# One softmax reciprocal per attention unit: from a power on GpSimd to a reciprocal on VectorE

## The chip, the core and the metric

The kernel runs on one core of a Trainium2 chip. The metric is the device time of one launch in microseconds. The profile names the engines PE (TensorE), DVE (VectorE), ACT (ScalarE), POOL (GpSimd) and SP (SyncE, which issues most transfers); PEld is PE's loading of weights.

## The reference

Two layers of a bidirectional encoder over 512 tokens of width 1024, in float32. Each layer has three token mixers side by side (A, B and C), an output projection, and an MLP. What matters here is the softmax of the mixers:

```python
def one_block(qblk):
    s = jnp.einsum('bhgqd,bhkd->bhgqk', qblk, k, preferred_element_type=jnp.float32) * scale
    p = jax.nn.softmax(s, axis=-1)
    return jnp.einsum('bhgqk,bhkd->bhgqd', p.astype(v.dtype), v)
```

C has 8 query heads (2 key heads), B has 4 heads, and A has 4 heads of dilated window attention with a bias; in the kernel A is a softmax over all 512 keys too, with the log of the count of windows that hold a key added to its bias. The output of the three goes through `w_o`, then a layer norm, then the MLP and a second layer norm.

## The kernel before, in words

The instruction streams of the engines are written out by hand and run in parallel; they meet at semaphores alone. A semaphore name such as `exped` counts up through the kernel, and a wait asks for a count. Each engine runs its stream in order: what stands behind a waiting instruction waits as well. An outer loop of two runs the layers.

Attention is a pipeline over 64 units a layer. A unit is one of 16 heads (C, then A, then B) with one of 4 tiles of 128 query rows. All matrices are split into a high and a low part, and products are summed from two or three passes. At step s of the pipeline:

- PE computes the scores of unit s into one of 3 banks (L1438, L1439, or L1284 to L1286 for B), transposes the probabilities of unit s-3 (L1451) once `normed` says that they are ready and once `pt_ready` of unit s-6 frees the bank, and does half of the product with the values for the two units s-6 and s-5 (L1284 to L1286, with the tiles pt_hi and pt_lo).
- DVE takes the negated row maximum of unit s from the bank (L1034); for A it adds the bias from the tile `band` and takes the maximum in one operation (L1027) and negates it (L1031). Then it makes pt_lo of unit s-4 from the transposed bank and pt_hi (L1041). Once in four steps each it also prepares the low part of the next head's q (L1012) and of k (L1005, where a new key head begins) and of v (L1057), and evacuates the head's output (L1049, "y part" below).
- ACT computes exp of unit s with the row sum as accumulator (L687, the sum in `smax[:, s % 4, 1:2]`), then pt_hi of unit s-3 (L695), and the high parts for q, k, v and the output.
- POOL waits for `exped`, raises the row sum to the power -1 (L450, against the constant tile `mone`), waits for its own result, multiplies the 128x512 tile of probabilities with it (L452) and signals `normed`.

`prob` and `smax` have 4 buffers each. The tile `band` has one, which SP loads for each of A's heads after the last maximum of the head before it. Around attention, PE works through weight slabs that ACT and DVE split into high and low parts.

Of the kernel before, what the change touches and what calls it, by code (L numbers as in the profile page):

```python
# [29 lines left out]
P = 128  # L30
KT = D // P
TT = S // P
# [44 lines left out]
UNITS = NH * TT  # L77
# [20 lines left out]
def trunk(nc, t_in, out, scratch):  # L98
# [3 lines left out]
    with ExitStack() as ctx:  # L102
# [37 lines left out]
        msq = keep("msq", [P, TT, 16])  # L140
        rms = keep("rms", [P, TT, 16])
        mhalf = keep("mhalf", [P, 16])
        mone = keep("mone", [P, 1])
        smax = keep("smax", [P, 4, 4])
        tmp = keep("tmp", [P, 2, S])
        u0 = cursor[0]
# [65 lines left out]
        def sem(name):  # L212
# [30 lines left out]

        k_hi_done, head_hi, head_ready, v_hi_done, v_ready = map(
            sem, ("k_hi_done", "head_hi", "head_ready", "v_hi_done", "v_ready"))
        scored, maxed, exped, normed, transposed, pt_hi_done, pt_ready, pv_done, y_hi_done, y_ready = map(
            sem, ("scored", "maxed", "exped", "normed", "transposed", "pt_hi_done", "pt_ready",
                  "pv_done", "y_hi_done", "y_ready"))
        h2_ready, acc_zero = sem("h2_ready"), sem("acc_zero")

# [145 lines left out]
        def _(pool):  # L396
            steps = [0]
# [8 lines left out]
            pool.memset(ones[:, :], 1.0).then_inc(setup_pool, 1)  # L406
            pool.memset(mhalf[:, :], -0.5).then_inc(setup_pool, 1)
            pool.wait_ge(setup_pool, 3)
            pool.memset(mone[:, :], -1.0).then_inc(setup_pool, 1)
            pool.affine_select(out=ident[:, :], in_=ones[:, :], compare_op=ALU.is_equal, fill=0.0, base=0,  # L410
                               pattern=[[-1, P]], channel_multiplier=1).then_inc(setup_pool, 1)
            pool.memset(lnrow[:, 0, :], 1.0).then_inc(setup_pool, 1)
            pool.memset(lnrow[:, 1, :], 0.0).then_inc(setup_pool, 1)
            pool.wait_ge(setup_pool, 7)
            PER = 2 * TT + TT + 2 * TT + UNITS + 2 * TT + 2 + 4
            with pool.Fori(0, DEPTH) as l:
                steps[0] = 0

# [26 lines left out]
                    j = 10 + n // TT  # L445
                    inv_sqrt(rms[:, n % TT, j:j + 1], msq[:, n % TT, j:j + 1], 1, brstd_done)
                for u in range(UNITS):
                    wait_apart(pool, exped, l * UNITS + u + 1)
                    p = prob[:, u % 4, :]
                    step(pool.tensor_tensor(smax[:, u % 4, 2:3], smax[:, u % 4, 1:2], mone[:, :], ALU.pow))  # L450
                    wait_apart(pool, pool_step, l * PER + steps[0])
                    pool.tensor_scalar(p, p, smax[:, u % 4, 2:3], 1.0, ALU.mult, ALU.mult).then_inc(normed, 1)  # L452
                for t in range(TT):
                    wait_apart(pool, var_ready, l * 8 + t + 1)
# [337 lines left out]
        def _(dve):  # L792
            steps = [0]
# [40 lines left out]
            with dve.Fori(0, DEPTH) as l:  # L834
# [181 lines left out]
                for s in range(ATT_STEPS):  # L1016
                    if s < UNITS:
                        m, h = HEADS[s // TT]
                        dve.wait_ge(scored, l * UNITS + s + 1)
                        if s >= 4:  # L1020
                            dve.wait_ge(exped, l * UNITS + s - 3)
                        if m == "A":
                            qt = s % TT
                            if qt == 0:
                                dve.wait_ge(band_in, (l * 4 + h + 1) * 16)
                            wait_apart(dve, transposed, l * UNITS + s - 3)
                            step(dve.tensor_tensor_reduce(prob[:, s % 4, :], bank[s % 3][:, :],  # L1027
                                                          band[:, 384 - P * qt:896 - P * qt], 1.0, -3.0e38,
                                                          ALU.add, ALU.max, smax[:, s % 4, 3:4]))
                            settle()  # L1030
                            dve.tensor_scalar(smax[:, s % 4, 0:1], smax[:, s % 4, 3:4], -1.0, None, ALU.mult  # L1031
                                              ).then_inc(maxed, 1)
                        else:
                            dve.tensor_reduce(smax[:, s % 4, 0:1], bank[s % 3][:, :], AX.X, ALU.max, negate=True  # L1034
                                              ).then_inc(maxed, 1)
                    u = s - LO_LAG
                    if 0 <= u < UNITS:
                        half = u // 2
# [209 lines left out]
        @block.tensor  # L1248
        def _(pe):
            pe.sem_inc(slab_free, RING)  # L1250
            pe.wait_ge(setup_pool, 5)

            def mod_cols(dst, src):

# [353 lines left out]
```

## Time and profile before

| | |
|---|---|
| median of 3 runs | 1533.49 us (1531.55 to 1535.78) |
| the profiled execution | 1535.78 us |
| its span in the profile | 1534.0 us |
| PE busy | 1347.1 us, 88% |
| DVE busy | 1080.8 us, 70% |
| ACT busy | 598.7 us, 39% |
| POOL busy | 360.4 us, 23% |

The span runs from the first to the last instruction that the profile shows. Busy shares are means over stages that have different limits, so the stretch in question has to be read by itself. In the chain of waits each piece is followed back from the last instruction to what released it; only work on that chain sets the end.

### The profile page before, as it was taken

How to read it: one execution, taken by the hardware profiler on the slowest of the kernel's cores; microseconds unless marked ns; L12 is line 12 of the kernel's file. 1: busy time of each engine (PE TensorE's matmuls, PEld its weight loads, DVE VectorE, ACT ScalarE, POOL GpSimd, SP SyncE). 2: the span in 40 equal slices, each digit the busy share in tenths (PEclk: the TensorE clock that was granted, in tenths of full speed). 3: DMA queues.
4: the chain of work that ended last, by engine and by line, in shares of the span. 5: the costliest groups of instructions: out<-in, count | busy, mean ns of one | idle time of the engine just before them, and what ended most of it. 6: DMA issues, size and time to landing. Idle time of an engine off the chain costs nothing.

```text
span 1534.0 us, 23304 instructions
## 1 busy us (share of the span) xinstructions
PE 1347.1 (88%) x6728; PEld 1133.7 (74%) x6728; DVE 1080.8 (70%) x1702; ACT 598.7 (39%) x1216; POOL 360.4 (23%) x411
## 2 busy tenths in 40 slices
PE   4598998899789999999929999979977999999992
PEld 2498777787668888887829977758766888888782
DVE  6957779877866555655777777988688655645668
ACT  0245478761422222221223647878132222222221
POOL 0504056540610000000361403756043000000024
PEclk9899989899889999999969999999998999999996
DMA  8654510104323332334325473010422333333431
GB/s 290 241 186 153 195 41 7 32 8 131 97 93 125 118 123 90 124 124 148 104 68 194 121 239 102 1 37 1 138 83 90 124 109 111 116 123 123 150 97 55
DMA packets 91844, 173.09 MB, mean 113 GB/s; under 512 B 8093, under 2 KB 18717, under 8 KB 91737
## 3 DMA queue, kind: packets, MB, share of 16 engines
q1 hardware_dynamic: 91208, 169.74, 34.2%
q10 hardware_dynamic: 528, 2.10, 0.4%
q8 instruction: 46, 0.75, 0.2%
q14 instruction: 62, 0.50, 0.1%
HBM read 167.61 MB, written 4.19 MB: 112 GB/s over the span
## 4 chain that ended last, share of the span: by engine, by line
PE 60%; DVE 18%; issue 10%; DMA 6%; ACT 3%; POOL 1%; DVEq 0%; SPq 0%; ACTq 0%; POOLq 0%
PE bank L1284 19%; PE bank L1285 19%; PE bank L1286 18%; DVE hT_hi L859 3%; DMA ada_w<-in_w_ada 2%; DVE ada_sum L807 1%; DVE slab_lo L851 1%; PE bank L1451 1%; DMA slab_raw<-in_w 1%; DVE smax L1034 1%; DVE pt_lo L1041 1%; DMA slab_raw<-in_w_in 1%; DVE X L1069 1%; DMA band<-bias_rows 1%; DVE tmp L1066 1%
## 5 line engine op out<-in xcount | busy, mean ns | idle before, releaser
L1284 PE MATMUL bank<-hT_hi,slab_hi 128*128 128x512 f32 x576 | 228.0, 396 | 22.9 <-DVE slab_lo L851 16.4
L1285 PE MATMUL bank<-hT_lo,slab_hi 128*128 128x512 f32 x576 | 226.5, 393 | 0.0
L1286 PE MATMUL bank<-hT_hi,slab_lo 128*128 128x512 f32 x576 | 226.3, 393 | 0.0
L1284 PE MATMUL bank<-slab_hi,h_hi 128*128 128x512 f32 x512 | 201.0, 393 | 6.3 <-ACT mod_a L778 6.3
L1286 PE MATMUL bank<-slab_hi,h_lo 128*128 128x512 f32 x512 | 199.4, 389 | 0.0
L1285 PE MATMUL bank<-slab_lo,h_hi 128*128 128x512 f32 x512 | 199.3, 389 | 0.0
L1284 PE MATMUL bank<-slab_hi,hT_hi 128*128 128x384 f32 (+3 forms) x448 | 155.8, 348 | 38.2 <-DVE slab_lo L851 20.2
L1121 DVE TENSOR_TENSOR slab_lo<-slab_raw,slab_hi 128x512 fp32r<-128x512 f32 x240 | 157.3, 711 | 21.7 <-ACT slab_hi L761 21.6
L807 DVE SCALAR_TENSOR_TENSOR ada_sum<-ada_w,c_col,ada_sum 128x512 f32<-128x512 f32 x196 | 146.8, 749 | 27.9 <-DMA ada_w<-in_w_ada 24.0
L467 POOL TENSOR_TENSOR acc<-acc,gate 128x512 f32<-128x512 f32 x8 | 13.8, 1722 | 648.9 <-DVE acc L1154 648.9
L1285 PE MATMUL bank<-slab_lo,hT_hi 128*128 128x384 f32 (+3 forms) x448 | 154.6, 345 | 0.0
L1286 PE MATMUL bank<-slab_hi,hT_lo 128*128 128x384 f32 (+3 forms) x448 | 154.5, 345 | 0.0
L851 DVE TENSOR_TENSOR slab_lo<-slab_raw,slab_hi 128x512 fp32r<-128x512 f32 (+3 forms) x144 | 96.1, 683 | 82.4 <-ACT slab_hi L507 82.2
L1284 PEld LDWEIGHTS bank<-hT_hi,slab_hi 128*128 128x128 f32 x576 | 109.8, 191 | 50.0 <-issue 27.2
L1154 DVE TENSOR_TENSOR acc<-bank,acc 128x512 f32<-128x512 f32 x112 | 69.5, 683 | 107.0 <-PE bank L1286 107.0
L507 ACT ACTIVATE slab_hi<-slab_raw 128x512 fp32r<-128x512 f32 (+3 forms) x144 | 73.1, 546 | 146.1 <-DMA slab_raw<-in_w_o 81.5
L1286 PEld LDWEIGHTS bank<-hT_hi,slab_lo 128*128 128x128 f32 x576 | 109.5, 190 | 23.2
L1285 PEld LDWEIGHTS bank<-hT_lo,slab_hi 128*128 128x128 f32 x576 | 109.9, 191 | 22.6
L1127 DVE TENSOR_TENSOR sqr<-relu 128x512 f32<-128x512 f32 x64 | 43.9, 686 | 112.5 <-ACT relu L765 101.3
L1284 PEld LDWEIGHTS bank<-slab_hi,hT_hi 128*128 128x128 f32 x448 | 87.0, 194 | 46.7 <-issue 24.7
L1284 PEld LDWEIGHTS bank<-slab_hi,h_hi 128*128 128x128 f32 x512 | 96.1, 188 | 29.4 <-ACT mod_a L778 9.8
L450 POOL TENSOR_TENSOR smax<-smax,mone 128x1 f32<-128x1 f32 x128 | 77.9, 609 | 166.2 <-ACT prob L687 165.8
(198 smaller groups left out, 2724.7 us busy)
## 6 DMA issues: line engine op xcount, KB each, us to landing
slab_raw<-in_w SPq DMA_DIRECT2D x256, 256.0 KB, 2.7
ada_w<-in_w_ada SPq DMA_DIRECT2D x56, 1024.0 KB, 5.6
slab_raw<-in_w_in SPq DMA_DIRECT2D x48, 192.0 KB, 3.6
slab_raw<-in_w_o SPq DMA_DIRECT2D x32, 256.0 KB, 2.7
slab_raw<-in_w_in SPq DMA_DIRECT2D x16, 256.0 KB, 5.2
lnrow<-in_ln_rows SPq DMA_DIRECT2D x8, 512.0 KB, 5.6
band<-bias_rows SPq DMA_DIRECT2D x8, 448.0 KB, 3.1
slab_raw<-in_w_in SPq DMA_DIRECT2D x16, 144.0 KB, 3.1
```

Of the source, the lines that this page charges most:

```text
L450: step(pool.tensor_tensor(smax[:, u % 4, 2:3], smax[:, u % 4, 1:2], mone[:, :], ALU.pow))
L507: act.activation(slab_hi[:, slot, 0:width], slab_raw[:, slot, 0:width], ACT.Copy).then_inc(slab_hi_done, 1)
L807: return dve.scalar_tensor_tensor(out=dst, in0=ada_w[:, k // 4, k % 4, :], scalar=c_col[:, 1, k:k + 1], in1=ada_b[:, :] if k == 0 else dst ...
L851: dve.tensor_tensor(slab_lo[:, slot, 0:width], slab_raw[:, slot, 0:width], f32(slab_hi[:, slot, 0:width]), ALU.subtract).then_inc(slab_lo_ ...
L859: step(dve.tensor_copy(hT_hi[:, k, :], tmp[:, k % 2, :]))
L1034: dve.tensor_reduce(smax[:, s % 4, 0:1], bank[s % 3][:, :], AX.X, ALU.max, negate=True).then_inc(maxed, 1)
L1121: dve.tensor_tensor(slab_lo[:, slot, :], slab_raw[:, slot, :], f32(slab_hi[:, slot, :]), ALU.subtract).then_inc(slab_lo_done, 1)
L1127: step_g(dve.tensor_tensor(sqr[:, f % 2, :], relu[:, f % 2, :], relu[:, f % 2, :], ALU.mult))
L1154: dve.tensor_tensor(dst, set_[t][:, :], dst, ALU.add).then_inc(evac_dve, 1)
L1284: pe.matmul(dst, a_hi, w_hi, start=first, stop=False)
L1285: pe.matmul(dst, a_hi, w_lo, start=False, stop=False)
L1286: return pe.matmul(dst, a_lo, w_hi, start=False, stop=last)
```

## The change

The reciprocal of the row sum moves from POOL to DVE. POOL loses the power and the wait for it, and the constant tile `mone` with its memset; it waits for a new semaphore, `summed`, in place of `exped`. DVE gains, at step s, behind the maximum of unit s and ahead of pt_lo, a reciprocal for unit s-1 with a wait for `exped` and one for `normed` of the unit that used the same buffer before. The counts of setup steps are adapted. Tiles behind `mone` move by 32 bytes.

```diff
-        mone = keep("mone", [P, 1])
...
-            pool.memset(mone[:, :], -1.0).then_inc(setup_pool, 1)
...
-            pool.wait_ge(setup_pool, 7)
-            PER = 2 * TT + TT + 2 * TT + UNITS + 2 * TT + 2 + 4
+            pool.wait_ge(setup_pool, 6)
+            PER = 2 * TT + TT + 2 * TT + 2 * TT + 2 + 4
...
                 for u in range(UNITS):
-                    wait_apart(pool, exped, l * UNITS + u + 1)
+                    wait_apart(pool, summed, l * UNITS + u + 1)
                     p = prob[:, u % 4, :]
-                    step(pool.tensor_tensor(smax[:, u % 4, 2:3], smax[:, u % 4, 1:2], mone[:, :], ALU.pow))
-                    wait_apart(pool, pool_step, l * PER + steps[0])
                     pool.tensor_scalar(p, p, smax[:, u % 4, 2:3], 1.0, ALU.mult, ALU.mult).then_inc(normed, 1)
...
                             dve.tensor_reduce(smax[:, s % 4, 0:1], bank[s % 3][:, :], AX.X, ALU.max, negate=True
                                               ).then_inc(maxed, 1)
+                    u = s - 1
+                    if 0 <= u < UNITS:
+                        dve.wait_ge(exped, l * UNITS + u + 1)
+                        if u >= 4:
+                            dve.wait_ge(normed, l * UNITS + u - 3)
+                        dve.reciprocal(smax[:, u % 4, 2:3], smax[:, u % 4, 1:2]).then_inc(summed, 1)
                     u = s - LO_LAG
...
-            pe.wait_ge(setup_pool, 5)
+            pe.wait_ge(setup_pool, 4)
```

## Rows read from the trace of the kernel before

**Rows 1.** The page: busy time by engine, and the chain by engine.

```profile
PE 1347.1 (88%) x6728; PEld 1133.7 (74%) x6728; DVE 1080.8 (70%) x1702; ACT 598.7 (39%) x1216; POOL 360.4 (23%) x411
...
PE 60%; DVE 18%; issue 10%; DMA 6%; ACT 3%; POOL 1%; DVEq 0%; SPq 0%; ACTq 0%; POOLq 0%
```

**Rows 2.** The power's line (durations min/median/max), and who waited for the multiplication.

```profile
L450 POOL TENSOR_TENSOR smax<-smax,mone x128: 538/551/1063, 203.5 to 1067.3; 128x1 f32<-128x1 f32 x128
...
  PEld bank L1451: 10.2, 14
```

**Rows 3.** Busy time by stretch: length, PE, PEld, DVE, ACT, POOL, PE clock, DMA.

```profile
222.00:259.00 37.00, 33.45 (x237) 28.38 (x236) 35.38 (x55) 32.08 (x74) 25.93 (x39) 1.00 0.00 1
```

**Rows 4.** Chain at both ends of attention (start, us, what); waits, 938 to 960.

```profile
203.11 0.20 ACT prob L687
...
204.23 1.02 POOL prob L452
...
215.08 0.52 DVE smax L1034
...
329.93 0.68 ACT prob L687 x2
...
331.80 0.70 POOL prob L452
...
PEld bank L1451 <- POOL prob L452: 4.3, 5, 1.4
```

**Rows 5.** Chain by line: 238 to 254 (C), 258 to 276 (A), 305 to 320 (B).

```profile
by line: issue 28.7%; DVE smax L1034 18.1%; DVE pt_lo L1041 13.2%; ACT pt_hi L695 9.2%; ACT prob L687 7.8%; ACT k_hi L666 7.2%; DVE q_hi L1012 6.1%; DVE k_lo L1005 4.3%; DVE hT_lo L1049 4.2%; DVEq L1019 0.8%; DVEq L1021 0.7%; ACT hT_hi L703
...
by line: issue 25.9%; DMA band<-bias_rows 17.0%; DVE prob L1027 12.8%; DVE k_lo L1005 11.7%; DVE pt_lo L1041 7.2%; ACT k_hi L666 7.1%; PE bank L1284 3.7%; DVE smax L1031 2.8%; ACT pt_hi L695 2.7%; ACT prob L687 2.4%; PE bank L1285 2.4%; PE 
...
by line: PE bank L1284 26.3%; PE bank L1285 25.0%; PE bank L1451 24.8%; PE bank L1286 24.4%
```

**Rows 6.** Timeline of one unit in C, from exp to its transposes.

```profile
228.67 0.20 ACT L687 ACTIVATION_READ_ACCUMULATOR prob<-bank,smax 128x1 f32 x1
...
228.91 0.69 DVE L1034 TENSOR_REDUCE smax<-bank 128x1 f32<-128x512 f32 x1
...
229.80 0.70 POOL L452 TENSOR_SCALAR prob<-prob,smax 128x512 f32<-128x512 f32 x1 [0.21 <-POOL smax L450]
...
231.03 0.60 PE L1451 MATMUL bank<-ident,prob 128*128 128x128 f32 x4
```

**Rows 7.** Small DVE operations; DVE's wait for the band.

```profile
L798 DVE RECIPROCAL c_col<-c_col x1: 203/203/203, 3.9 to 3.9; 128x8 f32<-128x8 f32 x1
...
269.95 0.69 DVE L1027 CUSTOM_DVE_ANT_0 prob<-bank,band 128x512 f32<-128x512 f32 x1 [1.84 <-DMA band<-bias_rows]
...
285.24 0.15 DVE L1031 TENSOR_SCALAR smax<-smax 128x1 f32<-128x1 f32 x1
285.31 0.68 DVE L1041 TENSOR_TENSOR pt_lo<-bank,pt_hi 128x512 fp32r<-128x512 f32 x1
```

**Rows 8.** Timeline of DVE and POOL in steady C.

```profile
231.64 1.21 POOL L452 TENSOR_SCALAR prob<-prob,smax 128x512 f32<-128x512 f32 x1 [0.49 <-POOL smax L450]
...
238.30 0.69 POOL L452 TENSOR_SCALAR prob<-prob,smax 128x512 f32<-128x512 f32 x1 [0.21 <-POOL smax L450]
...
238.60 0.93 DVE L1012 TENSOR_TENSOR q_hi<-qC,q_hi 64x512 fp32r<-64x512 f32 x1
...
240.76 0.68 DVE L1034 TENSOR_REDUCE smax<-bank 128x1 f32<-128x512 f32 x1
241.59 0.69 DVE L1041 TENSOR_TENSOR pt_lo<-bank,pt_hi 128x512 fp32r<-128x512 f32 x1
...
243.03 0.69 DVE L1034 TENSOR_REDUCE smax<-bank 128x1 f32<-128x512 f32 x1
243.75 0.69 DVE L1041 TENSOR_TENSOR pt_lo<-bank,pt_hi 128x512 fp32r<-128x512 f32 x1
```

**Rows 9.** Timeline of DVE in B: the maximum of one unit and its wait.

```profile
313.97 0.69 DVE L1034 TENSOR_REDUCE smax<-bank 128x1 f32<-128x512 f32 x1 [0.27 <-PE bank L1286]
```

More of the change, by code:

```diff
@@ L245, in trunk @@
             sem, ("k_hi_done", "head_hi", "head_ready", "v_hi_done", "v_ready"))
-        scored, maxed, exped, normed, transposed, pt_hi_done, pt_ready, pv_done, y_hi_done, y_ready = map(
-            sem, ("scored", "maxed", "exped", "normed", "transposed", "pt_hi_done", "pt_ready",
+        scored, maxed, exped, summed, normed, transposed, pt_hi_done, pt_ready, pv_done, y_hi_done, y_ready = map(
+            sem, ("scored", "maxed", "exped", "summed", "normed", "transposed", "pt_hi_done", "pt_ready",
                   "pv_done", "y_hi_done", "y_ready"))
```

## The prediction

> **What bounds the kernel now.** The page's busy shares come first: PE 88%, DVE 70%, POOL 23%, and in its chain of waits PE holds 60%, DVE 18%, POOL 1% [rows 1]. So all of POOL that stands on the chain is 1% of 1534.0 us, some 15 us, and only a part of POOL's work is touched. The costliest groups come next: the power (L450) runs 128 times, at 551 ns median, and PE's loads waited for L452 10.2 us in 14 places [rows 2]. That is a ceiling for what a shorter POOL chain can return by itself.
>
> The change touches attention alone, in layer 1 the heads C until about 259 us, A until 299, B until 331; layer 2 repeats them. Busy time by stretch gives DVE 35.38 of the 37.00 us of steady C, PE 33.45 [rows 3]. The last view is the chain inside each stretch. At the start of C it runs exp, power, multiplication, transposes, and PE from there to about 215 us [rows 4]. In steady C (238 to 254 us) DVE leads it: the maximum 18.1%, pt_lo 13.2%, with pt_hi and exp of ACT between [rows 5]. In A it is DVE with the load of the band (DMA, 17.0%), in B PE alone [rows 5]. So DVE, the engine that receives work, is the one that sets the pace in most of C and A, and POOL, the one that gives it up, does so at the start and the end of an attention stage only.
>
> **The change part by part.**
>
> *Removed from POOL.* Per unit the power, 0.55 us, and the hand-over to the multiplication, 0.21 us, as the row of the multiplication gives it [rows 2, 6]. In steady state this lies beside other work. Take one unit of C: exp's accumulator is read at 228.87, the multiplication starts at 229.80 and ends at 230.50, and the transposes of that unit begin at 231.03, 0.5 us after it [rows 6].
>
> *Added to DVE.* A reciprocal of 128x1 behind the maximum of the next unit and ahead of pt_lo. The wait on exped can't hold DVE: pt_lo already waits for pt_hi(u-3), which ACT issues behind the very exp(u) that the reciprocal waits for. The wait on normed is for a multiplication four units back. But two waits and one instruction more pass the queue of DVE; behind them stand pt_lo (PE's second product waits for it), the head's q, k, v and y parts, and the next maximum.
>
> In the unit above, the next maximum runs from 228.91 for 0.69 us. The reciprocal, started under its end at 229.51, would end near 229.66 and the multiplication start near 229.87, against 229.80 now [rows 6]. So the normed value comes neither sooner nor later in C. In A it comes later: where DVE stands for the band (the operation of 269.95 waited 1.84 us for DMA [rows 7]) the reciprocal is behind that operation. The unit's transposes wait for pt_lo of the same DVE step anyway, which the trace has 0.07 us behind the small operation, so at most the difference, 0.15 + 0.21 + 0.70 against 0.07 + 0.68, some 0.3 us, shows on PE, three times a layer, and DVE's own chain doesn't wait for it soon. I count zero.
>
> *Its price.* The trace has no 128x1 reciprocal. The nearest: a RECIPROCAL of 128x8, 203 ns; the 128x1 TENSOR_SCALAR of L1031, 154 ns, behind which pt_lo starts 0.07 us later (285.24, 285.31) [rows 7]. Ends: nothing (fully hidden) and 0.20 us on the path; I take 0.08, because the L1031 row is the same shape in the same place.
>
> The Trainium skill speaks against cheap small operations: VectorE: DVE Perf Modes, section on the TRN2 errata, says that each instruction pays a fixed latency of about 150 cycles at 0.96 GHz as measured, an estimated 0.16 us. The L1031 row agrees with that as a duration (0.154 us) but shows half of it under the next operation. By the page the term below would be 52 x 0.16 = 8.3 us in place of 4.2 and the time 1539.4 us; the row decides here.
>
> *How many count.* In a C cycle of four units the chain passes from the maximum directly to pt_lo in two, of which 243.03 to 243.75 is one. In the third (240.76 to 241.59, 0.83 us) pt_lo waits for ACT, which covers 0.08; the fourth is bypassed through ACT's exp [rows 8]. The first 12 or so units of C run at PE's pace, the chain comes to DVE at 215.08 [rows 4]. That leaves 20 units, half of them counted: 10 a layer. In A three of four units count, the fourth lies in the idle time ahead of the band: 12 a layer. In B the chain is PE's alone [rows 5], but DVE's own idle time there is small, 0.27 us ahead of the maximum at 313.97, one such wait in four units [rows 9], and four reciprocals take 0.32: I count a quarter, 4 a layer. Sum: 26 x 2 x 0.08 = **+4.2 us**. The bounds: 0, and 52 x 0.20 = 10.4.
>
> *Moved.* The multiplication now always starts about 0.36 us (0.15 + 0.21) behind the start of the reciprocal, and the q or k part of the head about 0.77 us (0.07 + 0.70) behind it. Such operations, with both inputs in SBUF, are delayed when they meet it: at 238.60 the q part took 0.93 in place of the 0.69 of its neighbours, the multiplication having begun at 238.30. Where both began together, at 231.64, it was the multiplication that took 1.21 us [rows 8]. From 238.60 the hold ends 0.54 us into the multiplication (0.30 + 0.24). In the new place that leaves 0.54 + 0.36 - 0.77, some 0.13 us of delay: less than C pays now where it pays, and more than A pays, whose such parts I find at about 0.69. Of the 8 such parts of A and layer some two lie in DVE's waits for the band: 6 x 0.13 = 0.8. C gains 0.24 - 0.13 at about three of its parts, 0.3. So 0.5 a layer, **+1.0 us** for both. Bounds: -1 and, at 0.24 for each of 8 parts in A and 8 in C and layer, 7.7.
>
> The Trainium skill gives a harder rule: SBUF — State Buffer, Who interferes with whom, says that the loser of the pair shared by DVE and GpSimd blocks fully. By that rule the estimate would be 0.29 us at each of the 8 parts of A and layer, 4.6 us in all. The row of 0.93 us shows less than the whole overlap of 0.39 us as delay (0.24), so the sum keeps to the row.
>
> *Given back.* At the start of attention the chain has exp to 203.31, multiplication at 204.23: 0.92 us. New: 0.05 + 0.15 + 0.21 = 0.41, and the multiplication, 1.02 us there because it meets a q part, may get 0.3 shorter. In layer 2 PE's loads wait for POOL five times in this start, 4.3 us in all [rows 4]. I take 1.0 a layer, bounds 0.5 and 2. At the end exp to 330.61, multiplication at 331.80 [rows 4], 1.2 us against 0.41; since the last transposes wait for an earlier pt_lo too, I take 0.7. Both layers: -2.0 - 1.4 = **-3.4 us**; bounds -2.4 and -5.4.
>
> *Setup and addresses.* One POOL memset less and a 32-byte shift of later buffers; the setup waits for DMA and DVE, not for POOL. Zero.
>
> **Sum.** 4.2 + 1.0 - 3.4 = +1.8 us. Against the profiled execution (span 1534.0, 1.8 around it, 1535.78) this gives 1537.6; that execution is the slowest of the three, 2.3 above the median 1533.49, so the forecast is 1533.49 + 1.8 = **1535.3 us**, no change that a measurement can tell (0.3%, or 4.6 us).
>
> **Rivals.**
> - *Every DVE step pays* (slower). The maxima, pt_lo and the reciprocal form one serial loop with ACT in C and A, so all 96 units of them count: 96 x 0.08 = 7.7, with the other terms +5.3, 1538.8 us; at 0.154 each +12.4, 1545.9. For it: DVE's 35.38 of 37.00 us in steady C [rows 3]. Against: ACT and PE have waits of their own. It decides from 0.135 us per counted unit, or 88 units at 0.08.
> - *Meetings on the port* (slower). Each q and k part of A and C loses 0.24: +7.7 in place of +1.0, 1542.0 us. For it: the phase of reciprocal and multiplication becomes fixed. Against: 238.60 and 231.64 show that a phase of a few tenths decides who pays [rows 8].
> - *POOL's relief wins* (faster). If the reciprocal hides as pt_lo's own wait does and all of PE's 10.2 us behind L452 go, 1523.3 us; with half the DVE price still paid 1525.4. It decides where the relief exceeds DVE's cost by 4.6 us. For it: layer 2's start, where POOL's 0.55 + 0.21 + 0.70 us a unit is the pace. Against: in C and A PE's waits are for pt_lo, not for POOL.
> - *It does nothing*: both sides hidden, 1533.5 us; in the middle case.
>
> **How the numbers follow.** Forecast and nothing together 0.60; every step pays 0.19; meetings 0.08; relief 0.13. Faster 0.13, same 0.60, slower 0.27. The forecast's own range is 1530 to 1538; for 8 in 10 it reaches into both sides, to 1528 below (part of the relief) and 1544 above (most of the first rival).
>
> **What would show it.** Right: a RECIPROCAL of 128x1 x128 on DVE near 0.16 us, with pt_lo 0.07 us behind it; POOL busy down by 78 us; no wait of PE's transposes for POOL in either start; C and A each longer by 0.5 to 1.5 us a layer, B alike, the first 20 us of attention shorter by about 1. Wrong: if the maximum-to-pt_lo distance in C grows by over 0.15 us in all four units, if q and k parts of 0.93 us become the rule, if waits for the multiplication appear at the transposes in A, or if the start gains over 2 us a layer.

## The result and the profile after

| | before | after |
|---|---|---|
| median | 1532.52 us (1531.27 to 1535.78, 4 runs) | 1545.17 us (1540.72 to 1549.59, 4 runs) |
| ratio | | 1.0088 [1.0064, 1.0111] |
| span of the profile | 1534.0 us | 1541.4 us |

The profile of before is of its slowest run and that of after of one below its median, so spans show less than the ratio. The ratio means 13.5 us more (9.8 to 17.0). The forecast was +1.8, "no change that a measurement can tell", and its wide range ended at 1544: the prediction was wrong in the size. The kernel became slower by 0.9%, clear of the noise.

The page after, busy time and the chain by engine (it answers to [rows 1]):

```profile
PE 1351.1 (88%) x6728; PEld 1129.0 (73%) x6728; DVE 1092.3 (71%) x1830; ACT 598.9 (39%) x1216; POOL 284.4 (18%) x282
...
PE 58%; DVE 19%; issue 10%; DMA 6%; ACT 4%; POOL 1%; DVEq 1%; SPq 0%; ACTq 0%; POOLq 0%
```

POOL gave up 76 us of work (78 were forecast) and DVE took 11.5. What the prediction does not have: PE, which has the same 6728 products as before, is busy for 4.0 us more.

The stages show where the time went. Their marks are read in the profile by line: the first and last operation with the band (the A heads), and the first and last of the relus that ACT runs in the MLP's loop. The rows of layer 1, first of before and then of after:

```profile
L1027 DVE CUSTOM_DVE_ANT_0 prob<-bank,band x16: 680/691/693, 258.3 to 298.1; 128x512 f32<-128x512 f32 x16
...
L765 ACT ACTIVATE relu<-bank x28: 592/599/601, 458.6 to 730.3; 128x512 f32<-128x512 f32 x28
```

```profile
L1023 DVE CUSTOM_DVE_ANT_0 prob<-bank,band x16: 674/691/693, 253.5 to 295.3; 128x512 f32<-128x512 f32 x16
...
L761 ACT ACTIVATE relu<-bank x28: 591/600/602, 453.5 to 728.7; 128x512 f32<-128x512 f32 x28
```

The A heads take 41.8 us where they took 39.8, and the MLP's loop takes 275.2 where it took 271.7. The second number is the surprise. No instruction of the MLP was touched, and attention has long ended when it begins. The same division for all kernels of the study, in us per layer (layer 1 / layer 2), each from its own profile, from start to start. C runs from the first maximum to the first negated maximum of A (L1031 in before, 0.7 us behind the first band operation), A from there to the last such negation, B from there to the last transpose. The MLP runs from its very first relu, which stands on a line ahead of the loop, to its last:

| kernel | C | A | B | MLP |
|---|---|---|---|---|
| before | 57.3 / 57.2 | 39.7 / 38.2 | 34.1 / 33.7 | 293.6 / 293.5 |
| after | 57.4 / 57.4 | 41.8 / 41.8 | 33.8 / 33.8 | 297.1 / 297.2 |
| e1_pad | 57.4 / 57.4 | 43.0 / 41.8 | 33.8 / 33.9 | 293.7 / 293.4 |
| e2_shift | 57.3 / 57.4 | 40.2 / 39.4 | 33.9 / 33.6 | 296.9 / 296.9 |
| e3_h2 | 57.3 / 57.5 | 40.5 / 39.3 | 33.3 / 33.7 | 297.2 / 296.8 |
| e5_all32 | 57.3 / 57.3 | 39.5 / 38.5 | 33.6 / 34.0 | 293.4 / 293.6 |
| e6_h2_128 | 57.3 / 57.4 | 39.4 / 39.5 | 33.7 / 33.6 | 296.9 / 296.6 |
| e4_dummy | 57.5 / 57.4 | 41.4 / 40.4 | 33.3 / 33.4 | 297.2 / 297.2 |
| e9_clean | 58.1 / 57.4 | 41.4 / 41.6 | 33.4 / 33.4 | 293.6 / 293.5 |
| e7_late | 57.7 / 58.6 | 40.8 / 39.5 | 34.2 / 34.6 | 293.4 / 293.6 |
| e8_nopow | 56.5 / 56.5 | 41.2 / 41.8 | 32.7 / 32.7 | 293.3 / 293.7 |
| e10_band2 | 57.3 / 57.4 | 33.8 / 33.5 | 33.4 / 33.4 | 293.3 / 293.3 |
| e14_clean2 | 57.4 / 58.0 | 34.2 / 34.6 | 33.4 / 33.4 | 293.5 / 293.6 |
| e15_nopow2 | 56.5 / 56.5 | 34.1 / 33.5 | 32.4 / 32.5 | 293.3 / 293.7 |
| e12_pad2 | 57.4 / 57.3 | 35.4 / 35.2 | 33.7 / 33.8 | 293.7 / 293.4 |
| e11_late2 | 58.6 / 57.8 | 33.7 / 33.6 | 34.2 / 34.2 | 293.4 / 293.6 |
| e13_ident | 57.4 / 57.4 | 33.5 / 33.5 | 33.4 / 33.4 | 293.5 / 293.3 |

One profile is one execution, and the A column scatters by a microsecond where nothing of attention's work was changed: before, e2, e3, e5 and e6 have before's attention, with A between 38.2 and 40.5, mean 39.4 of ten. A part of this scatter goes with the clock granted to TensorE. As a mean over the A stage, of its two levels, it is 0.82 in layer 1 of before (A 39.7) and 0.96 in layer 2 (38.2). It is not what sets the kernels apart: after has 0.88 in both layers and 41.8, the second layers of e2 and e3 have 0.87 and 39.4. The MLP column doesn't scatter: it is either 293.5 or 297, with a granted clock of 1.00 in all of them.

What an MLP product costs is read from PE's timeline. Three products of w2 of before, and three of after:

```profile
463.05 0.39 PE L1284 MATMUL bank<-slab_hi,h_hi 128*128 128x512 f32 x1
...
464.41 0.39 PE L1284 MATMUL bank<-slab_hi,h_hi 128*128 128x512 f32 x1
...
465.09 0.39 PE L1284 MATMUL bank<-slab_hi,h_hi 128*128 128x512 f32 x1
```

```profile
462.99 0.39 PE L1286 MATMUL bank<-slab_hi,h_hi 128*128 128x512 f32 x1
...
464.39 0.39 PE L1286 MATMUL bank<-slab_hi,h_hi 128*128 128x512 f32 x1
...
465.09 0.40 PE L1286 MATMUL bank<-slab_hi,h_hi 128*128 128x512 f32 x1
```

Nine products lie from the first to the last row of each. Before they take 2.04 us, 227 ns each; after 2.10 us, 233 ns each. PE doesn't idle in between; each product takes 6 ns more. (A row's own 0.39 us is longer: the next one starts before it ends.) The groups by shape for 470 to 690 us say which products (of before, then of after; the last columns are busy us and mean ns):

```profile
L1284 PE MATMUL bank<-hT_hi,slab_hi 128*128 128x512 f32 x160 | 62.2, 389 | 0.0
...
L1286 PE MATMUL bank<-slab_hi,h_lo 128*128 128x512 f32 x159 | 61.9, 389 | 0.0
```

```profile
L1286 PE MATMUL bank<-hT_hi,slab_hi 128*128 128x512 f32 x160 | 62.2, 389 | 0.0
...
L1288 PE MATMUL bank<-slab_hi,h_lo 128*128 128x512 f32 x153 | 60.4, 395 | 0.0
```

In the names the moving tile comes first and the stationary tile second. The products of w1 (hT moving, a slab stationary) are as fast as ever; those of w2 (a slab moving, h2 stationary) are slower. A layer has 8 groups of 96 products of w2, so 768 x 2 x 6.2 ns is 9.5 us at most if PE is the bound in all of them. The marks show 7.1 us inside the loops and 0.6 us behind the last relu of the program.

Back in attention, the steps of the prediction can be looked up. DVE in an A head, first a q part of before, then after:

```profile
263.07 0.69 DVE L1012 TENSOR_TENSOR q_hi<-qkA,q_hi 64x512 fp32r<-64x512 f32 x1
```

```profile
257.42 0.15 DVE L1027 TENSOR_SCALAR smax<-smax 128x1 f32<-128x1 f32 x1
257.50 0.16 DVE L1037 RECIPROCAL smax<-smax 128x1 f32<-128x1 f32 x1
257.58 0.67 DVE L1043 TENSOR_TENSOR pt_lo<-bank,pt_hi 128x512 fp32r<-128x512 f32 x1
258.28 0.81 DVE L1008 TENSOR_TENSOR q_hi<-qkA,q_hi 64x512 fp32r<-64x512 f32 x1
...
266.43 0.92 DVE L1001 TENSOR_TENSOR k_lo<-qkA,k_hi 64x512 fp32r<-64x512 f32 x1
```

POOL in the same stretch:

```profile
257.87 0.69 POOL L448 TENSOR_SCALAR prob<-prob,smax 128x512 f32<-128x512 f32 x1 [2.51 <-DVE smax L1037]
...
266.12 0.69 POOL L448 TENSOR_SCALAR prob<-prob,smax 128x512 f32<-128x512 f32 x1 [3.64 <-DVE smax L1037]
```

And the waits of PE's transposes in the A heads (254 to 298 us; before has no such line in this stretch):

```profile
PEld bank L1453 <- POOL prob L448: 4.7, 4, 2.1
PE bank L1453 <- POOL prob L448: 3.2, 3, 1.6
```

The reader is to see three things. The reciprocal takes 0.16 us, and pt_lo begins 0.08 us behind it: the price per instruction is right. The multiplication begins 0.37 us behind the reciprocal (257.50, 257.87), as forecast. But a q part is now 0.81 and a k part up to 0.92, against 0.67 to 0.69 for every one of these in A before; the k part meets the multiplication 0.31 us after that began, the same meeting as that of 238.60 in [rows 8]. And PE's transposes wait for the multiplication in A, which the prediction had priced at nothing and named as a sign of being wrong.

### The profile page after: what moved, and what is told of

Same layout as the page of the kernel before. It is cut to its first block, busy times and chain, and to the rows that moved or that the text cites. A ratio compares the mean times of both kernels' runs of the same rounds, so it can differ in the third digit from the quotient of the medians.

```text
span 1541.4 us, 23167 instructions
## 1 busy us (share of the span) xinstructions
PE 1351.1 (88%) x6728; PEld 1129.0 (73%) x6728; DVE 1092.3 (71%) x1830; ACT 598.9 (39%) x1216; POOL 284.4 (18%) x282
## 3 DMA queue, kind: packets, MB, share of 16 engines
q1 hardware_dynamic: 91208, 169.74, 33.9%
## 4 chain that ended last, share of the span: by engine, by line
PE 58%; DVE 19%; issue 10%; DMA 6%; ACT 4%; POOL 1%; DVEq 1%; SPq 0%; ACTq 0%; POOLq 0%
PE bank L1286 19%; PE bank L1288 18%; PE bank L1287 18%; DVE hT_hi L855 3%; DMA ada_w<-in_w_ada 2%; DVE smax L1030 2%; DVE pt_lo L1043 1%; DMA slab_raw<-in_w 1%; DMA band<-bias_rows 1%; DVE ada_sum L803 1%; DVE slab_lo L847 1%; DVE X L1071 1%; DVE k_lo L1001 1%; DVE tmp L1068 1%; DVE prob L1023 1%
## 5 line engine op out<-in xcount | busy, mean ns | idle before, releaser
L1288 PE MATMUL bank<-slab_hi,h_lo 128*128 128x512 f32 x512 | 202.1, 395 | 0.0
L448 POOL TENSOR_SCALAR prob<-prob,smax 128x512 f32<-128x512 f32 x128 | 92.6, 724 | 272.4 <-DVE smax L1037 272.2
L1286 PEld LDWEIGHTS bank<-slab_hi,h_hi 128*128 128x128 f32 x512 | 96.0, 187 | 32.4 <-ACT mod_a L774 9.7
```

Of the source, the lines that this page charges most:

```text
L1286: pe.matmul(dst, a_hi, w_hi, start=first, stop=False)
L1288: return pe.matmul(dst, a_lo, w_hi, start=False, stop=last)
```

## The experiments

Fifteen kernels, all timed beside the kernel before. Every ratio is to the kernel before as timed in the same session.

**Is it the 32 bytes? (e1_pad, e2_shift, e3_h2, e4_dummy)** The change shifts every tile behind `mone` by 32 bytes. e1_pad is the changed kernel with the place kept:

```diff
+        pad = keep("pad", [P, 1])
         smax = keep("smax", [P, 4, 4])
```

> The change, with an unused 32-byte tile in the place of mone, so that every later tile stands where it stood before. Address theory: the w2 products of the MLP return from 233 to 227 ns from start to start, the MLP gets 3.5 us shorter a layer (from its first relu operation at 431.6 to its last at 728.7 us, 297.1, back to 293.5) and the time is about 8 to 9 us below the changed kernel, near 1537 us, some 4 to 6 us above the kernel before. DVE theory (rival): the whole loss is the reciprocal's work and port meetings in attention, addresses do nothing; the time stays at 1545 us, 0.8% above before.

Measured: 1537.47 us, ratio 1.0063 [1.0038, 1.0087]. The MLP is back at 293.5. So the shift is real. What is left in attention costs some 0.6%, 9.6 us (5.8 to 13.3), by the ratio; its own profile has attention longer by 3.2 us a layer. The ratio alone would not prove the address: its interval overlaps that of after, and the medians of the two, 7.7 us apart, are from two sessions. The MLP column does.

e2_shift is the kernel before with nothing but the shift:

```diff
-        mone = keep("mone", [P, 1])
...
+        mone = over("mone", [P, 1], 93696)
```

> The kernel before, with POOL's power as it was, but with the tile mone placed behind all others, so that smax, tmp and all later tiles move down by 32 bytes. Address theory: the MLP is 3.5 us a layer longer, heads B about 0.5 us a layer, in all 8 to 9 us slower (0.5 to 0.6%), with no change to the order of work. DVE theory: no change at all.

Measured: 1539.76 us, 1.0064 [1.0042, 1.0085]. By the ratio the shift alone costs as much as the moved reciprocal does; the MLP is at 296.9. The expected 0.5 us a layer in B did not come (33.9 and 33.6).

e3_h2 is the kernel before with only the two h2 tiles moved, and the other way:

```diff
-        h2_hi = over("h2_hi", [P, 2, 4, S], 0, F32R)
-        h2_lo = over("h2_lo", [P, 2, 4, S], 16384, F32R)
+        h2_hi = over("h2_hi", [P, 2, 4, S], 32, F32R)
+        h2_lo = over("h2_lo", [P, 2, 4, S], 16384 + 32, F32R)
```

> The kernel before with the two tiles h2_hi and h2_lo alone 32 bytes further up; they are the stationary side of the w2 products. If the cost sits where PE loads its weights from an address that is 32 modulo 64, this one edit makes the MLP 3.5 us a layer longer, 7 us in all, and leaves attention as it was. If it sits in the tiles that ACT and DVE read and write (relu, sqr, acc), no change. Rival, DVE theory: no change.

Measured: 1537.11 us, 1.0051 [1.0032, 1.0071], MLP 297. Two tiles, 32 bytes up in place of down, and the whole loss of the MLP is there.

e4_dummy leaves POOL alone and gives DVE its 128 reciprocals for nothing:

```diff
+        spare = keep("spare", [P, 4, 4])
...
+                    u = s - 1
+                    if 0 <= u < UNITS:
+                        dve.wait_ge(exped, l * UNITS + u + 1)
+                        if u >= 4:
+                            dve.wait_ge(normed, l * UNITS + u - 3)
+                        dve.reciprocal(spare[:, u % 4, 2:3], smax[:, u % 4, 1:2]).then_inc(summed, 1)
```

> The kernel before, POOL's power and multiplication as they were, with DVE's 128 reciprocals added at the place of the change into an unused tile (64 bytes, so later tiles stay at 0 modulo 64). It measures what DVE's added instructions and waits cost without a change to when POOL multiplies. If DVE's own time is the larger part of what attention loses (0.08 us in 96 to 128 units): +5 to +8 us. If most of it is the meeting of the multiplication with the q and k parts, whose phase is not fixed here: +1 to +4 us. My first sum would have given +4.2 us.

Measured: 1543.42 us, 1.0093 [1.0065, 1.012]. This run is no test of DVE's work alone: its 64-byte tile had moved h2 by 64 bytes, and the MLP was at 297.2. It serves as one more address run, by accident, and e9_clean repeats it properly.

**Which rule of addresses? (e5_all32, e6_h2_128)** e5 moves the whole arena (`start = 1216 + 32`), so that every tile has a new address and no distance changes. e6 moves h2 by 128 bytes in place of 32.

> The kernel before with its whole arena 32 bytes further up: every tile's address changes, no distance between two tiles does. Relative theory (PE is slower where the tile that it loads as weights and the tile that it streams do not lie at the same place modulo some hundred bytes: equal modulo 256 in the kernel before, 32 or 64 off in the slow ones): the MLP stays at 293.5 us a layer. Absolute theory (a weight tile must lie at 64 modulo 128): h2 goes to 96 modulo 128 and the MLP to 297 us a layer, 7 us slower in all.

> The kernel before with h2_hi and h2_lo 128 bytes further up, at 64 modulo 128 as before, but 128 off modulo 256 against the slabs. Absolute theory: the MLP stays at 293.5 us a layer. Relative theory modulo 128 or less: the same; relative theory modulo 256 or more: 297 us a layer.

Measured: e5 1529.18 us, 0.9996 [0.9977, 1.0015], MLP 293.5. e6 1538.07 us, 1.0051 [1.0034, 1.0068], MLP 296.9 and 296.6. So 32 bytes of absolute address make no difference, and a shift of 128 bytes is about as bad as one of 32 (232 and 233 ns a product). In before, slab_hi lies at byte 66752 of a partition and h2_hi at 134848, both 192 over a multiple of 256. Shifts of 32 (e3), -32 (after, e2), 64 (e4) and 128 (e6) from that relation are slow. That a shift of 256 is fast again is shown by e12_pad2, below.

**What does the moved reciprocal cost in attention? (e7_late, e8_nopow, e9_clean)** e7 is e1 with the reciprocal behind DVE's other work of the step; e8 takes the power away from POOL and gives DVE nothing.

```diff
-                    u = s - 1
-                    if 0 <= u < UNITS:
...
                         dve.tensor_tensor(v_lo[:, KV[i] % 2, :, :], v_src(i), f32(v_hi[:, KV[i] % 2, :, :]),
                                           ALU.subtract).then_inc(v_ready, 1)
+                    u = s - 1
+                    if 0 <= u < UNITS:
```

> The change with the 32-byte pad, and DVE's reciprocal at the end of its step, behind pt_lo and the parts for q, k, v and y. The multiplication then meets DVE's maximum, which reads PSUM, and no q or k part: if the meetings (0.12 us a q part, 0.24 us a k part by the trace of the changed kernel) are what A loses beside the reciprocal's own 0.08 us, A gets about 1 us a layer shorter than with the pad alone (41.8 and 43.0). If the later normed value binds PE's transposes, which wait for the multiplication 3 to 4 times in A of the changed kernel, A and C get longer, several us in all. I expect the second, 2 to 8 us slower than the pad alone.

```diff
-                    step(pool.tensor_tensor(smax[:, u % 4, 2:3], smax[:, u % 4, 1:2], mone[:, :], ALU.pow))
-                    wait_apart(pool, pool_step, l * PER + steps[0])
-                    pool.tensor_scalar(p, p, smax[:, u % 4, 2:3], 1.0, ALU.mult, ALU.mult).then_inc(normed, 1)
+                    pool.tensor_scalar(p, p, smax[:, u % 4, 1:2], 1.0, ALU.mult, ALU.mult).then_inc(normed, 1)
```

> The kernel before without the power: POOL multiplies at once with the row sum in place of its reciprocal (this part of the computation is left out), DVE has nothing added. It shows what relief of POOL alone is worth, with tiles where they were: by my terms -3.4 us (first and last units of attention), and up to -10 us if all of PE's waits for POOL go; nothing if PE's start is bound otherwise.

Measured: e7 1534.86 us, 1.0033 [1.0017, 1.0049]; e8 1530.27 us, 0.9996 [0.9979, 1.0013]. e8 leaves the reciprocal out, so what it computes is no softmax any more; it serves for its time alone. In e7 a k part of A takes what it took in before:

```profile
271.00 0.68 DVE L1038 TENSOR_TENSOR pt_lo<-bank,pt_hi 128x512 fp32r<-128x512 f32 x1
271.60 0.67 DVE L1002 TENSOR_TENSOR k_lo<-qkA,k_hi 64x512 fp32r<-64x512 f32 x1
```

There are no meetings at all. The loss is about half of e1's, where 2 to 8 us more than e1's had been expected, and it has moved: A is at 40.8 and 39.5, but C is 0.4 to 1.3 longer and B 0.5 to 0.9. e8 is the upper bound of what POOL's relief can return, and it is nothing that could be measured, against the 3.4 us expected: C and B are shorter by about 0.8 and 1.0 us a layer, and A is longer by 2. The A heads lose time even where DVE gets no work. Two k parts a layer take 1.07 us there (267.42 and 279.61 in layer 1), as they begin 0.2 to 0.3 us behind a multiplication that now comes earlier, and A's multiplications take 0.9 to 1.0 us more in sum. That called for a look at what A has and the others don't, the loop over the single band tile.

e9 is e4 with the unused tile behind all others (`spare = over("spare", [P, 4, 4], 93696)`), so that nothing moves.

> The kernel before, GpSimd and every address as they were, with VectorE's 128 added reciprocals writing into an unused tile that lies behind all others (nothing is moved by it). Theory 'two causes' (addresses in the second part of a layer, VectorE's added step in the attention): first to last relu 293.5 us a layer, not the 297.2 of the run with the unused tile in the middle; the attention 1.0 to 1.5 us a layer longer than before, so 2 to 3 us in all: ratio 1.0013 to 1.002. Rival 'the longer second part comes from the work, by way of when its slabs arrive': 297.2 again and a ratio near 1.009.

Measured: 1534.18 us, 1.0023 [1.0004, 1.0043], with the MLP at 293.6 and 293.5. The longer MLP was the address, not the work. A is at 41.4 and 41.6, 2.1 us above the mean of the five kernels with before's attention: more than 16 x 0.08 = 1.3, and attention as a whole is 2.2 us a layer longer, where 1.0 to 1.5 was expected.

**Is it the band loop? (e10_band2, e12_pad2, e11_late2)** A second band tile in the place of C's q, which is free by then. The band of A1 and A3 goes there, each load is one head earlier, and each tile has its own semaphore:

```diff
+        band2 = over("band2", [P, 896], 8192)
...
+                            elif h == 1:
+                                wait_apart(sp, head_ready, l * NH + 8)
                             else:
-                                wait_apart(sp, maxed, l * UNITS + 4 * (8 + h))
+                                wait_apart(sp, maxed, l * UNITS + 4 * (7 + h))
...
-                            sp.dma_start(band[:, :], src).then_inc(band_in, 16)
+                            sp.dma_start((band2 if h % 2 else band)[:, :], src
+                                         ).then_inc(band2_in if h % 2 else band_in, 16)
```

> The kernel before with a second band tile, in the place of the C heads' q, so that the band of heads A1 and A3 is loaded while the head before is still at work, and that of A2 two heads ahead. Theory 'the A heads are paced by the loop last maximum of a head, band load, first band op of the next': the three waits of about 1.8 us per layer go, and what of them is on the path shortens the A stage by 2 to 5 us a layer: ratio 0.993 to 0.997. Rival 'TensorE has work in hand during those waits': the A stage stays at 39.5 and 38.5 us, ratio 0.999 to 1.001.

Measured: 1517.21 us, ratio 0.9898 [0.9869, 0.9927]. That is 15.6 us less than before by the ratio, 13.2 by the medians, and more than was expected. The stages give 6.1 us a layer. First the band's rows in A of before and of after, layer 1:

```profile
L346 SPq DMA_DIRECT2D band<-bias_rows x3: 320/320/344, 266.7 to 289.2; - x3
...
  DMA band<-bias_rows: 3.6, 2
  PE bank L1439: 2.6, 2
...
DMA to landing us min/median/max: 3.1/3.2/3.2
```

```profile
L345 SPq DMA_DIRECT2D band<-bias_rows x3: 319/320/343, 261.6 to 285.7; - x3
...
DMA to landing us min/median/max: 3.1/3.2/3.8
```

Then those of e10:

```profile
L1032 DVE CUSTOM_DVE_ANT_0 prob<-bank,band x16: 676/692/693, 254.8 to 288.5; 128x512 f32<-128x512 f32 x16
L350 SPq DMA_DIRECT2D band<-bias_rows x3: 319/320/343, 243.2 to 272.3; - x3
...
  PE bank L1444: 0.6, 1
  PE bank L1456: 0.2, 1
...
DMA to landing us min/median/max: 3.0/3.2/3.3
```

The three loads in this stretch still take 3.2 us each, but nothing waits for them, and A's 16 operations span 33.7 us in place of 39.8 (38.2 in layer 2). The stage got shorter by some 5.8. In before DVE stands three times a layer ahead of a head's first band operation. The view puts two of these waits down to the band, 3.6 us, and the third, 1.95 us at 292.55, to PE. But the last load, issued at 289.15, took 3.19 us, and the operation starts 0.21 us behind its landing, exactly as in the other two. So all three end with the band: 5.5 us in layer 1 and 5.2 in layer 2, close to what the stage gave back. The clock doesn't explain the gain: layer 2 of before has 0.96 in A, e10 0.95, with 38.2 and 33.5 us. The pace of A before was the loop: last maximum of a head, load, first operation of the next.

e12 is the changed kernel with the place kept, the second band tile, and h2 256 bytes higher; e11 is e7 with the second band tile.

> The changed kernel with the 32 bytes kept (reciprocal where the change puts it), the second band tile, and the two h2 tiles 256 bytes higher. Second part of the layer: theory 'place modulo 256 bytes': 293.5 us from first to last relu; rival 'any other distance than the one of before is slow' or 'modulo 512 and more': 297 us, as with 32, 64 and 128 bytes. A stage: theory 'band loop': as in the kernel before with a second band tile, within 0.5 us; rival 'the meetings of VectorE and GpSimd on q and k parts, whatever the band does': 2 us a layer longer than there.

> The changed kernel with the 32 bytes kept, the reciprocal behind the other work of a VectorE step, and the second band tile. Theory 'VectorE's lost time is carried from head to head by the band loop': without the loop the reciprocal costs no more than 1 us in all against the kernel before with a second band tile (ratio 0.993 to 0.998 to the kernel before). Rival 'it costs in C and B too': C and B stages 0.5 to 1 us longer each, ratio 0.003 above that of the kernel before with a second band tile.

Measured: e12 1523.63 us, 0.9952 [0.9931, 0.9973]; e11 1520.44 us, 0.9923 [0.9895, 0.9952]. First the address. The w2 products of e12:

```profile
L1294 PE MATMUL bank<-slab_hi,h_lo 128*128 128x512 f32 x155 | 60.4, 390 | 0.0
L1293 PE MATMUL bank<-slab_lo,h_hi 128*128 128x512 f32 x155 | 60.3, 389 | 0.0
```

The mean is that of before, and the MLP is at 293.7 and 293.4. A distance of 256 bytes is fast, so as far as it was tried the relation is one modulo 256. Then A:

```profile
L1029 DVE CUSTOM_DVE_ANT_0 prob<-bank,band x16: 676/691/693, 257.5 to 292.9; 128x512 f32<-128x512 f32 x16
```

35.4 us, 1.65 above e10 as a mean of both layers: neither 0.5 nor 2, and nearer to the rival. In the ratios the change without the loop still costs 0.0054, some 8 us, hardly less than the 0.0063 of e1. The transposes' wait for the multiplication, 7.9 us in after, has shrunk to one line (250 to 300 us):

```profile
PEld bank L1459 <- POOL prob L454: 0.4, 1, 0.4
```

So it was the band's wait that made the normed values late. In e11, with no meetings, A is at e10's 33.7, and C and B each pay some 0.8 us instead, as the rival had it.

**The two prices without the loop (e14_clean2, e15_nopow2, e13_ident)** e14 is e9 and e15 is e8, each with the second band tile.

> VectorE's 128 added reciprocals into an unused tile behind all others, GpSimd as before, with the second band tile. Theory 'VectorE's added step costs by its own length, 0.08 us a unit, and the band loop made 2 us a layer of it': A stage 33.6 + 16 x 0.08 = 34.9 us at most, attention at most 1.5 us a layer above that of the kernel before with the second band tile (124.4): ratio 0.990 to 0.992. Rival 'each added step costs 0.16 us and more, with its waits': A stage 36 us, ratio 0.993 or above.

> No power on GpSimd and no reciprocal on VectorE (GpSimd multiplies by the row sum itself, the reciprocal is left out), with the second band tile. Theory 'the earlier multiplication meets q and k parts and costs what the meetings take': A stage 33.6 + up to 1.2 us, C and B 0.8 shorter each, attention 124.4 - 0.4: ratio 0.989 to 0.990. Rival 'the meetings are free, A's loss came by the band loop': A stage 33.6 or below, attention 1.5 us a layer shorter than with the power: ratio 0.987 to 0.988.

Measured: e14 1519.25 us, 0.992 [0.9899, 0.9942]; e15 1516.8 us, 0.9904 [0.9885, 0.9922]. e14 keeps to its theory (A 34.4, attention 1.1 us a layer above e10). In e15 attention is 1.6 us a layer shorter than in e10 and no q or k part of A is longer than 0.69, so it is the rival's picture; the ratio can't tell the two. With the other kernels this makes a table of the A stage (mean of the two layers, us):

| | one band tile | two band tiles |
|---|---|---|
| neither | 39.4 (five kernels) | 33.65 (e10) |
| DVE's step alone | 41.5 (e9), 40.9 (e4) | 34.4 (e14) |
| earlier multiplication alone | 41.5 (e8) | 33.8 (e15) |
| both | 41.8 (after), 42.4 (e1) | 35.3 (e12) |

Without the loop DVE's step costs 0.75 us a layer, which the prediction's 12 x 0.08 = 0.96 meets well. The earlier multiplication costs 0.15, and both together 1.65; the difference of 0.75 goes with the meetings, which of these only e12 has (q parts 0.81, k parts up to 0.93 as in after, 1.2 us a layer in sum). With the loop, either alone costs 1.5 to 2.1, and both together 2.4 to 3.0. So for the change itself the loop adds some 0.7 to 1.3 us a layer to a cost of 1.65 that is there without it.

The traces say where the loop's part lies. The A stage is the sum of four pieces: from the first band operation of a head to the issue of the next load, three times; the three loads; 0.21 us behind each landing; and the last head. From the five kernels with before's attention to after the mean of a layer goes from 39.4 to 41.8:

| | heads up to the issue | three loads | behind landings | last head |
|---|---|---|---|---|
| before's attention (five kernels) | 23.8 | 9.4 | 0.6 | 5.6 |
| after | 24.9 | 10.2 | 0.6 | 6.1 |
| e9 | 24.6 | 10.2 | 0.6 | 6.1 |
| e8 | 25.0 | 9.6 | 0.6 | 6.3 |

In after 1.6 us more lie in the heads' own work, as much as without the loop, and 0.7 in the loads: the second takes 3.8 us in both layers, and at most 3.34 in all ten layers with before's attention. In e9 the work is 1.3 longer, which is 16 x 0.08, and the loads 0.8. In e8 the loads are as they were. Why a load takes longer in some of these kernels is not shown.

e13 asks whether the rule on addresses holds for the transposes against the identity, another pair that breaks it (ident lies 96 over a multiple of 256, prob 192):

```diff
+        pad1 = keep("pad1", [P, 24])
         ident = keep("ident", [P, P])
+        pad2 = keep("pad2", [P, 40])
```

> The kernel before with the second band tile, and the identity tile moved up by 96 bytes to the same place modulo 256 bytes as the tiles that are transposed against it (all tiles behind it move by 256 bytes). Theory 'any pair of TensorE operands at different places modulo 256 bytes runs 3% slower': a transpose of an A head takes 1 to 2 ns less from start to start, under 1 us in all: ratio to the kernel before 0.989 to 0.990, as with the second band tile alone (0.9898). Rival 'transposes are hit harder than the 512-column products': 2 to 5 us in all, ratio 0.986 to 0.988.

Measured: 1519.61 us, 0.9921 [0.9897, 0.9944], not told apart from e10. The mean of a transpose is what it was; e10 and then e13, 220 to 300 us:

```profile
L1456 PE MATMUL bank<-ident,prob 128*128 128x128 f32 x156 | 23.8, 276 | 0.0
```

```profile
L1458 PE MATMUL bank<-ident,prob 128*128 128x128 f32 x160 | 24.5, 276 | 0.0
```

From start to start a transpose takes 109 ns in both, where the theory had 1 to 2 ns less. The rule was not seen there.

## Why the prediction was wrong, point by point

**The failed step: "Setup and addresses. One POOL memset less and a 32-byte shift of later buffers ... Zero."** The shift of addresses was the term put at nothing without a row and without a bound; the reason given, what the setup waits for, bears on the memset alone. The runs show 7.1 us in the two MLPs, 7.8 us [4.9, 10.9] by e3's ratio, and some 8 us with the last group: over half of the 13.5, and two thirds of the 11.7 us by which the forecast missed. With 8 us there the sum would have been +9.8 and the forecast 1543. No run tried the memset by itself.

**The rest of the miss is attention,** +2.5 us a layer by the stages where the terms add up to +0.9:

| us a layer | the prediction's terms | measured, after against the five kernels |
|---|---|---|
| C | 0.8 for steps, -0.3 meetings, -1.0 given back: -0.5 | +0.05 |
| A | 0.96 for steps, +0.8 meetings: +1.8 | +2.4 |
| B | 0.3 for steps, -0.7 given back: -0.4 | +0.1 |

So A was forecast nearly as it is without the loop (1.65, e12), and the two stages that were to give something back gave nothing.

**"In A it comes later ... I count zero."** What this missed is that A before was a loop with the band's load in it, although the chain of A in [rows 5] had DMA at 17.0% and the waits of 1.84 us in [rows 7] were counted as cover for the fourth unit. The 7.9 us in which PE's transposes wait for the multiplication in A belong to the same picture (0.4 us in e12). That the loop enlarges the cost is shown by the table of the A stage; 0.7 of the 2.4 us in after is a load that takes longer, and the cause of that stays open.

**The price of a reciprocal.** Right: 154 ns median, pt_lo 0.08 us behind it. Its line in after:

```profile
L1037 DVE RECIPROCAL smax<-smax x128: 142/154/166, 198.4 to 1072.2; 128x1 f32<-128x1 f32 x128
```

The Trainium skill's figure (VectorE: DVE Perf Modes, TRN2 errata, an estimated 0.16 us per instruction) fits the duration but not the step between two, which the timeline has at 0.08, and e14's A stage follows the smaller number.

**The units counted.** In A about right (e14: 0.75 for the 0.96). In C, 10 units and 0.8 us a layer, too many as it seems: C is 57.4 against 57.3 in after and e1. In e9 and e14 it is 57.4 in one layer and 58.0 in the other, and the longer one holds a q part of 1.05 to 1.08 us (212.13 in e9). In B, after is at 33.8, as the kernels with before's attention, although e8 is 1.0 us shorter there; four of B's parts take 0.92 us in after. How cost and gain cancel in C and B was not taken apart.

**"Moved".** The multiplication stands where it was forecast, and a q part pays 0.12 us, close to the 0.13. The k part of 266.43 pays 0.23, since it begins 0.59 us behind pt_lo and not 0.70, and so falls deeper into the multiplication. C did not gain, against the forecast of 0.3: its eight q parts take 1.0 us more than 0.69 each where they took 0.5 more. Summed over the timeline, the parts of A and C pay 1.7 us a layer, 3.4 in all, against the term of 1.0; on the A stage without the loop the meetings show as 0.75 a layer. The rule in the Trainium skill (SBUF — State Buffer, Who interferes with whom: the shared pair is an exclusive lock) again asks for more than the trace shows: at 266.43 the two lie together for 0.38 us, to 266.81, and the delay is 0.23.

**"Given back".** The start came as forecast: the first transposes are 0.8 us earlier in both layers. It is gone some 12 units later, when DVE sets the pace. e8 shows what a free reciprocal would return in C and B, 1.8 us a layer and so the 1.7 of the prediction, and that A took it all back. The size of the term was right for POOL's relief alone; in after C and B return nothing.

**The rivals.** "Meetings on the port" (1542.0) had a true mechanism at the wrong size; "every DVE step pays" (7.7 us for the step) has e9 against it, 3.5 us (0.6 to 6.6), and e14, whose ratio is 0.0022 above e10's, 3.4 us, with B as it was and C longer in one layer of two. The second says little by its ratio, since e13, of the same session as e14 and with e10's stages, lies 0.0023 above e10 too. "POOL's relief wins" fell with e8, at 0.9996 even without DVE's step. The largest cause, the addresses, was in no rival.

**The sum again**, from the profiles: 7.1 in the MLPs, about 1.2 for the two last groups of w2 (0.6 seen), 4.8 in A, 0.2 in C and B, together 13.3 us, against 13.5 measured. That this fits to 0.2 us is luck. The stretches left out of it scatter by microseconds from profile to profile: attention begins at 201.8 us in before, at 196.8 in after, and between 196.3 and 202.1 in kernels with before's addresses. The single ratios don't add as neatly: e3 and e1 together give 17 us, with intervals of 3 to 4 us on each.

**A kernel that beats both** is e10: the reciprocal left on POOL, h2 where it was, a second band tile. It takes 0.9898 of the time of before.

## What to carry to other kernels

Removing or adding a tile moves all tiles behind it, so give an edit's address shift a term and a bound of its own, and keep places fixed with a pad when something else is to be measured. Look at stages that the edit does not touch: a stage that repeats to half a microsecond tells more than the total. Where the chain of a stage shows a load (17% here) that is issued only when the tile is free, suspect that the loop is the pace: here small additions came out enlarged, and a second buffer was worth more than the rearrangement of the engines' work around it. A wait that the view puts down to an engine can be the load's all the same; compare it with the time of the landing.

## What the hardware showed that was not expected

A product of 128x128 with 512 columns repeated every 227 ns when its stationary tile (h2) and its moving tile (a slab) lay at the same place modulo 256 bytes in SBUF, and every 232 to 233 ns when they were -32, 32, 64 or 128 bytes from it (after, e3, e4, e6). At 256 bytes it was fast again (e12). Other distances were not tried. Moving both by 32 bytes changed nothing (e5). The rows call both tiles f32; the kernel declares them float32r. The transposes (128x128 against the identity) show no such effect, 276 ns both ways, and whether the scores and the products with the values would was not tried. Why the relative place matters is not shown.
